# State updates of the sample sequences moved between the output product's slots, in 32-row groups

## The reference, cut

```python
    for i in range(DEPTH):
        h = rmsnorm(x, W['norm_mix'][i])
        cp = h @ W['w_in'][i]
...
        x = x + jnp.concatenate([ya, yb, yc], axis=-1) @ W['w_out'][i]
        h = rmsnorm(x, W['norm_ffn'][i])
...
    # retention_chunked, per chunk (a sample sequence is one chunk of 8 tokens)
        S = S * c_decay[None, :, None, None] + jnp.einsum('blhk,blhv,hl->bhkv', kc, vc, k_decay)
...
    # retention_mixer
    out = out * lax.rsqrt(jnp.mean(out * out, axis=-1, keepdims=True) + RMS_EPS)
...
    # ssd_chunked, per chunk
        h = h * jnp.exp(last)[..., None, None] + jnp.einsum('blgr,blgrp,blgn->bgrpn', wk, xc, Bc)
```

## Time and profile before

| | us |
|---|---|
| runs (3) | 1372.06 to 1381.52 |
| median | 1377.24 |
| profiled execution | 1379.99 |
| its span, first to last instruction | 1378.2 |
| PE busy | 1319.0 |
| DVE busy | 931.0 |
| ACT busy | 713.5 |
| mean granted clock of PE | 0.935 |

### The profile page before, as it was taken

How to read it: one execution, slowest core, us unless ns; L and a number is a source line. 1 busy time by engine, 2 the same in 40 slices (tenths; PEclk the granted TensorE clock), 3 DMA queues, 4 the chain that set the end, 5 groups by cost and what they waited for, 6 DMA issues and landing times.

```text
span 1378.2 us, 26218 instructions
## 1 busy us (share of the span) xinstructions
PE 1319.0 (96%) x10139; PEld 1159.4 (84%) x10139; DVE 931.0 (68%) x1483; ACT 713.5 (52%) x1095; POOL 141.2 (10%) x165
## 2 busy tenths in 40 slices
PE   6999999989999999899999999889999999999996
PEld 6999887768999999889988776888788888788875
DVE  6585755445655555758676553558998898998996
ACT  6533353114443334373344421358777777787784
POOL 1121210030000000112122002000100100010010
PEclk9999998559999999999999955799999999999998
DMA  7221320035444444043122000728997997997993
GB/s 277 98 94 48 116 78 16 12 108 217 153 146 161 151 153 153 16 137 122 48 94 100 32 1 13 261 77 307 335 348 262 335 343 262 360 323 255 359 327 125
DMA packets 63063, 235.05 MB, mean 171 GB/s; under 512 B 7280, under 2 KB 7504, under 8 KB 62320
## 3 DMA queue, kind: packets, MB, share of 16 engines
q1 hardware_dynamic: 60192, 220.27, 45.3%
q0 software_dynamic: 2336, 12.81, 2.4%
q10 hardware_dynamic: 432, 0.52, 0.1%
HBM read 225.48 MB, written 8.09 MB: 169 GB/s over the span
## 4 chain that ended last, share of the span: by engine, by line
PE 48%; DVE 3%; ACT 3%; issue 2%; POOL 0%; DVEq 0%; ACTq 0%
PE bank L1315 8%; PE bank L1292 6%; PE bank L1294 5%; PE bank L1293 5%; PE bank L586 4%; PE bank L592 3%; PE bank L594 2%; PE bank L593 2%; PE bank L1212 2%; DVE wlo L1864 1%; ACT whi L1376 1%; PE bank L1077 1%; PE bank L1257 1%; PE bank L750 1%; PE bank L1241 1%
## 5 line engine op out<-in xcount | busy, mean ns | idle before, releaser
L1376 ACT ACTIVATE whi<-wraw 128x1024 fp32r<-128x1024 f32 x407 | 428.8, 1059 | 371.3 <-PE bank L594 309.2
L1864 DVE TENSOR_TENSOR wlo<-wraw,whi 128x1024 fp32r<-128x1024 f32 x407 | 494.8, 1229 | 185.6 <-ACT whi L1376 179.0
L592 PE MATMUL bank<-hh,whi 128*128 128x320 f32 x608 | 199.6, 328 | 15.3 <-DVE Dx L1955 4.5
L593 PE MATMUL bank<-hl,whi 128*128 128x320 f32 x608 | 191.0, 314 | 0.0
L594 PE MATMUL bank<-hh,wlo 128*128 128x320 f32 x608 | 190.9, 314 | 0.0
L1292 PE MATMUL bank<-whi,hh 128*128 128x512 f32 (+1 forms) x384 | 147.4, 384 | 3.4 <-DVE wlo L1864 3.0
L1294 PE MATMUL bank<-wlo,hh 128*128 128x512 f32 (+1 forms) x384 | 143.5, 374 | 0.0
L1293 PE MATMUL bank<-whi,hl 128*128 128x512 f32 (+1 forms) x384 | 143.2, 373 | 0.0
L592 PEld LDWEIGHTS bank<-hh,whi 128*128 128x128 f32 x608 | 117.3, 193 | 25.6 <-issue 11.0
L593 PEld LDWEIGHTS bank<-hl,whi 128*128 128x128 f32 x608 | 117.7, 194 | 0.0
L594 PEld LDWEIGHTS bank<-hh,wlo 128*128 128x128 f32 x608 | 117.2, 193 | 0.0
(11 more groups left out here) (423 smaller groups left out, 2292.8 us busy)
## 6 DMA issues: line engine op xcount, KB each, us to landing
wraw<-in_w SPq DMA_DIRECT2D x410, 512.0 KB, 4.9
smb<-in_s_ssm POOLq DMA_DIRECT2D x2, 1536.0 KB, 7.7
out_o_ssm<-smb POOLq DMA_DIRECT2D x2, 1536.0 KB, 11.5
cst<-in_consts SPq DMA_DIRECT2D x1, 2161.0 KB, 13.3
srw<-in_s_rwkv POOLq DMA_DIRECT2D x2, 768.0 KB, 5.5
out_o_rwkv<-srw POOLq DMA_DIRECT2D x2, 768.0 KB, 3.9
x<-in_x SPq DMA_DIRECT2D x2, 640.0 KB, 5.0
out_y<-x SPq DMA_DIRECT2D x4, 320.0 KB, 2.2
```

Source lines behind the costliest of these rows:

```text
L592: mm(out, hi, rh, start=first, stop=False)
L593: mm(out, hi, rl, start=False, stop=False)
L1376: af(whi[:, ring % HI, :], wraw[:, POS[ring], :], ACT.Copy).then_inc(S("slot_hi"), 1)
L1864: tt(wlo[:, POS[ring], :], wraw[:, POS[ring], :], whi[:, ring % HI, :].bitcast(F32), ALU.subtract).then_inc(S("slot_split"), 1)
```

## The change

On PE, retention's block 2 makes its state product last, after the norm's broadcast, and in halves: tokens 0 to 31 with sequences 0 to 3 into bank 4, tokens 32 to 63 with sequences 4 to 7 into bank 5. Mamba's late states leave the list; `late_product` makes them in the same halves, m_ = 0 and 1 behind output slot 1, 2 and 3 behind slot 2, into banks 0 to 5. ACT copies them to `ds` (six buffers) and POOL adds them to `smb`. Each output slot takes RWKV's and Mamba's k-tiles first and retention's last, and only slot 0's retention tiles wait for `rt_done`. The splits of output slots 0 and 1 go into the lists of ACT and DVE (`out`). POOL's first `rings_free` stands ahead of `Bwe`. `rs_over` goes into each side of the branch.

```diff
 PE (retention, block 2)
-                    if b == 2:
-                        m = mm(B[RT_BANKS[h // 2]][p, :], kd, vx[:, h, :, :], start=True, stop=True)
...
                 m.then_inc(S("rt_rb"), 1)
+                if b == 2:
+                    yield
+                    pe.wait_ge(S("rt_vx"), l + 1)
+                    pe.wait_ge(S("rt_o2"), l + 1)
+                    pe.wait_ge(S("rw_done"), 3 * (l + 1))
+                    for h in range(HB):
+                        p = slice(64 * (h % 2), 64 * (h % 2) + 64)
+                        for u, (r, seqs) in enumerate(HALF_SEQ):
+                            m = mm(B[RT_NEW_BANKS[u]][p, (h // 2) * 4 * HD:(h // 2 + 1) * 4 * HD],
+                                   vkt[r, 2 + h // 2, 64 * (h % 2):64 * (h % 2) + 64], vx[r, h, seqs, :], start=True, stop=True)
+                    m.then_inc(S("rt_dS"), 1)
...
+            def late_product(l, m_):
+
+                g = m_ // 2
+                if m_ == 2:
+                    pe.wait_ge(S("rt_S"), 3 * (l + 1))
+                elif m_ == 3:
+                    pe.wait_ge(S("mb_ds_used"), NSEQ * l + 2)
+                pe.wait_ge(S("mb_Bwe"), 2 * l + g + 1)
+                for z in range(2):
+                    for u, (r, seqs) in enumerate(HALF_SEQ):
+                        bk = LATE_BANKS[(2 * m_ + u) % len(LATE_BANKS)]
+                        m = mm(B[bk][:, z * 3 * HD:(z + 1) * 3 * HD], Bwe[g][r, seqs.start + 2 * (m_ % 2) + z, :],
+                               xw[r, 3 * g:3 * g + 3, :], start=True, stop=True)
+                m.then_inc(S("mb_ds"), 2)
+
+            def out_slot(l, j):
+
+                g, out = G_OUT[l] + j, B[6 + j % 2][:, 0:T]
+                pe.wait_ge(S("slot_split"), g + 1)
+                for at, k in enumerate(OUT_K):
+                    if j == 0 and k == TA:
+                        pe.wait_ge(S("rt_done"), 3 * (l + 1))
+                    m = three(out, k, g, hh[:, k, :], hl[:, k, :], at == 0, at == KT - 1)
+                m.then_inc(S("slot_used"), 1)
...
-                    full_slot(G_OUT[l] + j, G_OUT[l] + j, B[6 + j % 2][:, 0:T])
+                    if j == LATE - 1:
+                        pe.wait_ge(S("mb_ds_used"), NSEQ * (l + 1))
+                    out_slot(l, j)
+                    if j in (1, 2):
+                        late_product(l, 2 * j - 2)
+                        late_product(l, 2 * j - 1)
 ACT
+            def late_states(l, ks):
+
+                for k in ks:
+                    act.wait_ge(S("mb_ds"), NSEQ * l + 2 * (k // 2) + 2)
+                    if k >= LATE:
+                        act.wait_ge(S("gp_done"), late_at(l, k - LATE))
+                    af(ds[:, k % LATE, :], B[LATE_BANKS[k % LATE]][:, 0:2 * 3 * HD], ACT.Copy).then_inc(S("mb_ds_used"), 1)
...
                 for j in range(KT):
+                    if j in (2, 3):
+                        late_states(l, range(4 * j - 8, 4 * j - 4))
                     hi_ahead(G_OUT[l] + j)
 POOL
-                gp.wait_ge(S("mb_done"), 3 * (l + 1))
-                gp.sem_inc(S("rings_free"), 1)
                 gp.wait_ge(S("mb_ds"), NSEQ * (l + 1))
                 gp.sem_inc(S("rings_free"), 1)
                 gp.wait_ge(S("rw_Sp"), 4 * (l + 1))
                 out(p_rw[l], srw_p[:, :, :])
-                gp.wait_ge(S("mb_ds_used"), NSEQ * (l + 1))
+                for k in range(NSEQ):
+                    gp.wait_ge(S("mb_ds_used"), NSEQ * l + k + 1)
+                    s0 = HALF_SEQ[k % 2][1].start + 2 * (k // 2 % 2)
+                    f = smb[:, k // 4, s0:s0 + 2, :, :].rearrange("p s h c -> p (s h c)")
+                    tt(f, f, ds[:, k % LATE, :], ALU.add).then_inc(S("gp_done"), 1)
+                gp.wait_ge(S("gp_done"), late_at(l, NSEQ - 1))
                 gp.dma_start(o_mb[l], smb[:, :, :, :, :]).then_inc(S("ring_out"), 16)
```

116 lines of the change are left out of this document (56 added, 60 removed).

## The result

The changed kernel takes 1364.67 us (median of 20 runs, 1359.7 to 1376.29), the kernel before 1374.93 us (20 runs, 1369.29 to 1384.58): a ratio of 0.9933, 95% interval 0.9915 to 0.995. A second set of 12 runs gave 0.9934 (0.9901 to 0.9967). So the change gains 0.7%, 10 us, where I forecast 24. The time lies at the upper end of my range (1346 to 1366), but the gain fell where I had put a chance of 0.11.

What follows compares the result with a forecast made beforehand. PE, busy 96% of the span, was taken as the bound, with almost 20 us per layer at half clock before the output product. Gains of 12.5 + 13.8 + 1.6 = 27.9 us, less 4, gave 24: 1353 us, range 1346 to 1366.

Steps and rivals of the forecast that it cites:

- a chance of 0.11: Whole kernel: the forecast's probability that the change would land within 1% of the time before.
- steps 1 to 5: End of retention's square to the next phase: 12.5 us earlier in layer 0, 13.8 in layer 1, row groups side by side.
- step 6: Final norm: the last broadcast moves into the two branches and follows the reciprocal by 0.14 us, gaining 1.6 us.
- the ends for which I took 4 us off: Both layers: possible costs of a later clock rise, unhidden weight loads and changes of product form; 4 us off the gain.
- Step 1: Retention's norm in layer 0: state products no longer stand ahead, so the chain takes 2.03 us and PE is free at 289.9.
- step 7: Output phase side work on DVE, ACT and POOL, costed at nothing; POOL's eight additions 9.6 us, o_ssm hidden with 3 us spare.
- the sum of 27.9: Gains of layer 0, layer 1 and the final broadcast with row groups side by side: 12.5 + 13.8 + 1.6 us.
- rival on the clock: Late products behind slots 1 and 2: clock falls to 1.2 GHz, costing 12 us, 1365 us in all; chance under 1 in 10.
- rival of new waits in the output phase: Waits for o_ret in layer 1 and slot 6's weights give back 3 to 8 us, 1356 to 1361 us; 2 in 10.
- I am wrong if PE waits in slots 2 to 5 for x: Output phase: a sign named beforehand as refuting the forecast, which expected no PE idle time over 0.5 us in eight slots.

Runs made afterwards that it cites:

- e1: Changed kernel with POOL's eight additions into smb left out (states incomplete); 1353.39 us, 0.9853 of before.
- e5: Changed kernel with the late additions done by DVE straight from the banks, without ACT's copies and POOL's additions; 1351.13 us, 0.9802 of before.
- e6: e5 with each late product contracting all 64 rows of the sample block in place of 32; 1359.12 us, 0.9835 of before.
- e10: e5 with DVE's x addition ahead of its raw_lo and sum of squares; 1343.55 us, 0.9781 of before.
- e7: e5 with retention's state products and their four DVE updates ahead of the norm's sum and reciprocal again; 1354.64 us, 0.9818 of before.
- e9: e5 with all late products ahead of slot 0 and DVE's eight additions ahead of its first wlo; 1363.99 us, 0.987 of before.
- e16: Changed kernel with POOL's issue of RWKV's prompt-state transfer moved behind its eight additions; 1359.16 us, 0.9904 of before.
- e11: Changed kernel with POOL's run of eight additions waiting for DVE's x addition of slot 2; 1354.22 us, 0.9839 of before.
- e12: Changed kernel with POOL's run of eight additions waiting until DVE's raw_lo of tile 1 has ended; 1368.65 us, one run.
- e14: Changed kernel with DVE's x addition ahead of raw_lo and POOL's run of additions waiting for raw_lo of tile 1; 1351.58 us, one run.
- e4: Changed kernel with POOL's additions in pairs, each pair waiting for DVE's x addition of slots 1 to 4; 1358.05 us, 0.9865 of before.
- e2: Changed kernel with each of POOL's eight additions covering 192 of 384 columns (states incomplete); 1360.96 us, 0.9886 of before.

## Why the prediction came out as it did

**Right: where the time was, and the sum.** It put 12.5 and 13.8 us on the two layers (steps 1 to 5), a stretch of 102.05 - 26.3 = 75.8 us. Without the hold it is 76.1 (e1) and 75.3 (e5). In times, e1 and e5 lie 23 and 24 us under the runs of the kernel before beside them (intervals 13 to 28 and 15 to 40); I had 24. The steps one by one: the chain is 3.7 us from square to slot 0, of which 1.98 for the states (I had 1.84); a batch is 1.57 (1.35); the 1.4 us wait of layer 1 is gone; PE's last broadcast starts 0.05 us behind the reciprocal (step 6, 1.5 us of 1.6). The row groups do run side by side (e6). In e10, whose slots have no waits, a slot takes 3.52 us, the two with a batch behind them 5.11 and 5.21 and the one behind the second batch 3.62, so a batch costs 1.69 us, 0.34 over its columns. If the tiling mode costs something when it changes, as the Trainium skill, TensorEngine Tiling (Key Properties) has it, it is within that. So two of the ends for which I took 4 us off did cost something: two batches take 3.4 us a layer and not 2.7, and slot 0 took up to 6.17 us where before it took 5.2. The stretch comes out near the sum all the same: in e5 by its quick slots 0, in e10 because the small gaps between the slots are gone (before, slots 1 to 7 of layer 0 took 3.52 to 3.84 us each).

**Right size, other reason: the order around the norm.** Step 1 credits taking the states from ahead of the norm. e7 prices the order itself at 0.5 us a layer: once the states take 1.98 us, they hardly matter on either side. What step 1 removed was the long form of them, and what made up most of the 15 us was the late products (e9, e6).

**Wrong: step 7, the overlap that it took for free.** "Side work that I cost at nothing" gave POOL's eight additions 1.2 us each and asked only whether POOL would be done in time. It was, early: 0.96 us each, done at 312.2, o_ssm issued at 312.51. The step never asked whom the additions keep from working meanwhile. They cost 6.41 and 6.40 us of PE's waiting, and a second fall of the clock behind each wait: from slot 0 to the next phase layer 0 took 43.3 us against 33.7 in e5, 9.6 more, of which 6.4 are the wait, about 2.3 the half clock in slot 4, and 0.9 slot 0, where e5's clock rose sooner. In all 93.8 - 76.1 = 17.7 us: the sum of 27.9 less 17.7 is 10.2 us, against 10.3 between the medians. That they meet so closely is luck: 1.4 of the 17.7 lie in the slots 0, and the medians of the second set are 8.1 apart. The fall of the clock behind a wait wasn't in the prediction; its rival on the clock put the fall into the late products, where it stayed at 1.00. My rival of new waits in the output phase was of this kind, but named o_ret and the weights of slot 6, which cost nothing, and was too small by half. "I am wrong if PE waits in slots 2 to 5 for x" was the sign that came.

**It could have been asked.** The kernel before has a sign that POOL's work can keep DVE's from ending, at the start of layer 1 (DVE and POOL, times from the span's start). Two operations on 11 and 3 columns, 0.17 and 0.16 us in layer 0, last 1.47 and 1.40 us beside POOL's memsets, which follow straight on an issue:

```profile
584.95 0.54 POOL L2767 DMA_DIRECT2D cv_in<-in_s_conv  x1
585.48 0.28 POOL L2768 MEMSET srw_p<- 128x192 f32 x1
585.53 1.47 DVE L1979 TENSOR_SCALAR s_omu<-par 128x11 f32<-128x11 f32 x1
585.60 1.40 DVE L1980 TENSOR_SCALAR s_oka<-par 128x3 f32<-128x3 f32 x1
```

It is not the same case. These two read one tensor each, and beside the same memsets behind the same issue in layer 0 (8.34 to 10.02 us) two TENSOR_TENSORs with two SBUF operands, `sqb` from 8.62, take 1.07 us together, against 1.02 for the two ahead of the issue (6.52). So it shows that the question was worth asking, not what the answer would be; what a memset does to which operation no run here shows.

## What to carry to other kernels

Work that moves to GpSimd is not free because GpSimd is idle: ask which VectorE operations with two SBUF operands fall into its time, and who waits behind them. A long "normal" operation in a trace (8.43 us where its line takes 0.54 elsewhere) is the first thing to look for after such a move. If GpSimd must do it, issue the transfer behind the run (e16), or see to it that the run starts from a wait and not from the issue (e11, e12); other work between the two was not tried, and within the run it doesn't help, since the second to eighth additions hold VectorE too. Better, give the additions to the engine that reads the bank anyway, in one of its gaps.

## What the runs showed of the hardware

- While POOL adds SBUF tensors, a DVE operation with two SBUF operands waits, and POOL waits for DVE's. If POOL came to its run from a wait, they take turns by instruction: 1.28 us for a 0.5 us operation (0.89 behind one that reads a bank, e14), and the eight additions take 10.24 in place of 7.71 us. A DVE operation that reads a bank isn't touched (0.47 us in e11).
- If POOL goes straight from issuing a transfer into the run, DVE isn't let in before the run ends: 8.43, 8.21, 8.13, 8.42 us for eight additions, 5.18 for eight half ones, 2.73 for two, 1.75 for one, 5.28 for a `wlo` that asked in the middle (the same places in layer 1 are within 0.25 us of these). Why the issue has this effect no run here shows.
- The Trainium skill, SBUF — State Buffer (SBUF: two separate sides), has the port pair of the two engines as an exclusive lock: whichever starts first keeps it "for the whole instruction" and the other fully blocks. The turns of e11 agree with it; the holds over eight instructions don't follow from it, and there the measurement decides.
- The granted clock fell to 0.50 after PE had stood still for 6.4 us, in both layers, and stayed there for 5.7 us of dense work after the wait in layer 0 and 3.0 in layer 1; in the kernels whose waits were under 1 us (e1, e4, e5, e10, e14) it stayed at 1.00 from its rise in slot 0 up to the next phase. Between these it goes either way: e11's wait of 2.91 us left it at 1.00, e12's of 2.30 us was followed by 0.50, and of e2's two waits of 3.16 and 3.17 us only the second was.
- When the clock rises varies with the same work: 2.2 to 5.7 us after slot 0's start (e5's layer 1, the changed kernel's layer 1).
